# A four-stage encoder trunk: who normalises the tiles, gate-rank columns from whole x, a rounding moved, and the last norm's order

## The chip, the cores and the metric

One NeuronCore of a Trainium2 chip runs the whole program. The metric is the device time of one execution in microseconds (us).

## The reference, cut to what matters

x is 512 tokens by 1024 channels in float32. Two layers follow one another; each is a mixer and a SwiGLU network, and behind each of the four sublayers stands a norm over the channels:

```
x = layer_norm(ALPHA * x + mix(x), ln1_g, ln1_b)
x = layer_norm(ALPHA * x + swiglu(x), ln2_g, ln2_b)

h = x @ w_in                                   # even mixer
gq, gk, gv, ga, gr, sq, sk, sv = split(h)
log_a = log_sigmoid(ga @ w_a2 + b_a) / 16      # ga: 16 gate-rank columns
o = concat(gla(gq, gk, gv, log_a, gr), swa(sq, sk, sv)) @ w_out
```

The odd mixer is a gated DeltaNet with a causal convolution in front; of it only the 16 columns for beta and decay (ba) matter here.

## The kernel before, in words

**Number format.** Large products are made in three matmuls: each float32 operand is a rounded high part and a low remainder (w_hi, w_lo, x_hi, x_lo), and high x high, high x low and low x high are summed in one PSUM bank (mm3). ScalarE (ACT) rounds weights to w_hi, GpSimd (POOL) subtracts to get w_lo; both work piece by piece, two pieces to a block of 1 MB. There are two buffers for blocks, so a block may be rounded only when the block two before it is used up. The load of a block on the queue of SyncE (SP) waits for the low part of the block two before it. Only the 32 columns around the gate rank (ga) and around ba are multiplied in plain float32, by few_columns: eight contraction steps with x_hi, then eight with x_lo, in quarters of the array.

**Order.** Each engine's program is written out by hand. The eight PSUM banks are given out by unit_plan, and a result's first matmul waits until the bank's last content has been taken. TensorE (PE) computes in this order: sq, skv, gq, gk, ga, turned q and k (qT, kT), the gate matrix (a2), gv, then for each tile of 128 tokens scores, gr, attention and state; then the output projection mix, a norm, gate and up, down, a norm, and the odd layer likewise.

**The banks around gv.** qT, kT of four tiles, a2 and gv take banks in a ring. gv's tiles use banks 1, 2, 3 and 4, which held qT 1, kT 1, qT 2 and kT 2. The scores of tile 0 take banks 0 and 1, the turned k_d bank 2, and gr's tile 0 bank 3, which gv's tile 2 had. ScalarE empties all of these.

**x_tm and x_fm** are the input by tokens and by channels; they share their place in SBUF. x_fm is read at the start, x_tm is loaded over it and read by the first addition of ALPHA * x and the mixer's result.

**A norm between sublayers** (i = 1, 2, 3). For each of four tiles VectorE (DVE) adds x and the result (L1238), takes statistics of both halves (L1240, L1220); ScalarE takes the root (L841); VectorE the reciprocal (L1195), and then (x - mean) * rstd in two halves of 512 channels (L1211). The normalising of tile t - 1 is placed behind the statistics of tile t. TensorE turns each tile (turn_x, L1842, 8 transposes into 8 banks, one for each 128 channels; the last banks are those of the sublayer's last results). When the fourth tile has been turned, round_x makes x_hi and x_lo: it applies the norm's gain and bias by channel on the way out of PSUM. The first, second and third matmuls of the next block wait for it (fm_block with fresh). Just ahead of round_x, ScalarE rounds both pieces of the second weight block of the next stage.

**The last norm** (i = 4) goes to the output: VectorE computes (x - mean) * gain (L1201) and then * rstd + bias (L1206), in halves, and SP stores each half. TensorE finishes the first tile, after 12 more matmuls the second, and after 24 each the third and the fourth.

## Time and profile before

| | |
|---|---|
| median of 3 runs | 1242.6 us (1242.52 to 1243.76) |
| the profiled execution | 1242.73 us |
| its span | 1240.9 us |
| PE busy | 1226.9 us, 99% |
| DVE busy | 439.5 us, 35% |
| ACT busy | 450.8 us, 36% |
| POOL busy | 588.2 us, 47% |
| mean granted clock | 0.997 of full speed |

An engine's busy time is the union of its instructions; a matmul's duration overlaps that of the next, so the distance of two starts tells the rate. The chain of work that ended last gives PE 93% of the span and DVE 4%. In the timelines a row is: start, duration, engine, line, operation, result<-sources, how many merged, and in brackets how long the engine was idle before it and who released it.

### The profile page before, as it was taken

The page shows a single profiled execution, that of the slowest core. Times are in us where ns is not written, and L with a number is a line of the kernel's source. Part 1 is how long each engine was busy: PE and PEld are TensorE (multiplying, and loading weights), DVE is VectorE, ACT ScalarE, POOL GpSimd, SP SyncE. Part 2 cuts the span into 40 slices and gives each one's busy share as a digit, 9 for nine tenths or more (in the row PEclk, how much of TensorE's full clock was granted, in tenths as well). Part 3 has the DMA queues.
Part 4 walks back from the last instruction along what each step waited for, and adds up shares of the span by engine and source line. Part 5 has one row for each costly group of instructions (what it writes and reads, how often), then busy time and mean ns, then how long its engine had stood idle before and what let it go on. Part 6 is the DMA issues. An engine that isn't in the chain of part 4 may idle for free.

```text
span 1240.9 us, 17146 instructions
## 1 busy us (share of the span) xinstructions
PE 1226.9 (99%) x7108; PEld 1011.8 (82%) x7108; DVE 439.5 (35%) x772; ACT 450.8 (36%) x670; POOL 588.2 (47%) x280
## 2 busy tenths in 40 slices
PE   9999999999999999999999999999999999999997
PEld 7877887888888888887777888888788888888885
DVE  5556526201011100127779845654511011110105
ACT  4167825222223221215544455542532223221211
POOL 4243444943444343445744347444684444435341
PEclk9999999999999999999999999999999999999998
DMA  9322052333332333332243333124233322324221
GB/s 319 98 69 69 7 164 69 102 102 102 102 94 78 104 124 112 102 102 63 90 125 114 97 109 94 27 69 137 68 102 102 95 91 86 102 85 147 75 102 68
DMA packets 106065, 122.96 MB, mean 99 GB/s; under 512 B 18947, under 2 KB 80581, under 8 KB 105989
## 3 DMA queue, kind: packets, MB, share of 16 engines
q1 hardware_dynamic: 98244, 118.56, 29.9%
q10 hardware_dynamic: 7744, 3.32, 1.1%
q8 instruction: 56, 0.92, 0.3%
q14 instruction: 21, 0.16, 0.0%
HBM read 117.93 MB, written 3.70 MB: 98 GB/s over the span
## 4 chain that ended last, share of the span: by engine, by line
PE 93%; DVE 4%; ACT 1%; POOL 1%; DVEq 0%; ACTq 0%; issue 0%
PE bank L1666 26%; PE bank L1667 26%; PE bank L1668 26%; PE bank L2098 4%; PE bank L1697 1%; PE bank L1698 1%; PE bank L1710 1%; DVE stats L1240 1%; DVE x_tm L1238 1%; PE bank L1929 1%; PE bank L2207 1%; POOL w_lo L681 1%; PE bank L1732 1%; PE bank L2044 1%; PE bank L2190 0%; PE bank L1856 0%
## 5 line engine op out<-in xcount | busy, mean ns | idle before, releaser
L681 POOL TENSOR_TENSOR w_lo<-w_raw,w_hi 128x1024 fp32r<-128x1024 f32 (+1 forms) x200 | 470.6, 2375 | 545.8 <-ACT w_hi L816 520.9
L1666 PE MATMUL bank<-x_hi,w_hi 128*128 128x512 f32 x880 | 344.3, 391 | 0.0
L1667 PE MATMUL bank<-x_lo,w_hi 128*128 128x512 f32 x880 | 342.5, 389 | 0.0
L1668 PE MATMUL bank<-x_hi,w_lo 128*128 128x512 f32 x880 | 342.5, 389 | 0.0
L816 ACT ACTIVATE w_hi<-w_raw 128x1024 fp32r<-128x1024 f32 (+1 forms) x200 | 196.3, 1032 | 205.7 <-issue 160.4
L1666 PEld LDWEIGHTS bank<-x_hi,w_hi 128*128 128x128 f32 x880 | 165.1, 188 | 35.5 <-issue 0.8
L1668 PEld LDWEIGHTS bank<-x_hi,w_lo 128*128 128x128 f32 x880 | 165.2, 188 | 34.1
L1667 PEld LDWEIGHTS bank<-x_lo,w_hi 128*128 128x128 f32 x880 | 165.2, 188 | 33.9
L1247 DVE TENSOR_TENSOR f_ab<-bank,f_ab 128x512 f32<-128x512 f32 x44 | 30.4, 692 | 364.8 <-PE bank L1668 364.8
L1668 PE MATMUL bank<-w_hi,h_lo 128*128 128x512 f32 x352 | 136.9, 389 | 0.0
L1666 PE MATMUL bank<-w_hi,h_hi 128*128 128x512 f32 x352 | 136.9, 389 | 0.0
L1667 PE MATMUL bank<-w_lo,h_hi 128*128 128x512 f32 x352 | 136.9, 389 | 0.0
L1666 PE MATMUL bank<-w_hi,x_hi 128*128 128x512 f32 (+1 forms) x284 | 110.7, 390 | 0.7 <-POOL w_lo L681 0.7
L1238 DVE SCALAR_TENSOR_TENSOR x_tm<-x_tm,bank 128x512 f32<-128x512 f32 x32 | 22.0, 687 | 246.2 <-PE bank L1668 238.7
L1668 PE MATMUL bank<-w_hi,x_lo 128*128 128x512 f32 (+1 forms) x284 | 107.4, 378 | 0.0
L1667 PE MATMUL bank<-w_lo,x_hi 128*128 128x512 f32 (+1 forms) x284 | 107.3, 378 | 0.0
L864 ACT ACTIVATE h_hi<-f_ab 128x512 fp32r<-128x512 f32 x44 | 27.8, 632 | 187.4 <-DVE f_ab L1247 187.4
L859 ACT ACTIVATE f_ab<-bank 128x512 f32<-128x512 f32 x44 | 26.3, 598 | 144.8 <-PE bank L1668 140.5
L1666 PEld LDWEIGHTS bank<-w_hi,h_hi 128*128 128x128 f32 x352 | 66.1, 188 | 13.8
L1668 PEld LDWEIGHTS bank<-w_hi,h_lo 128*128 128x128 f32 x352 | 66.1, 188 | 13.8
L1667 PEld LDWEIGHTS bank<-w_lo,h_hi 128*128 128x128 f32 x352 | 66.1, 188 | 13.5
L1455 DVE SCALAR_TENSOR_TENSOR KH<-bank,convw,KH 128x511 f32<-128x511 f32 (+2 forms) x72 | 53.9, 749 | 26.4 <-ACT KH L1005 23.3
(297 smaller groups left out, 1257.9 us busy)
## 6 DMA issues: line engine op xcount, KB each, us to landing
w_raw<-ffn_w_gate_dram SPq DMA_DIRECT2D x22, 1024.0 KB, 5.3
w_raw<-ffn_w_up_dram SPq DMA_DIRECT2D x22, 1024.0 KB, 5.3
w_raw<-ffn_w_down_dram SPq DMA_DIRECT2D x20, 1024.0 KB, 5.0
w_raw<-od_w_in_dram SPq DMA_DIRECT2D x16, 1024.0 KB, 5.8
w_raw<-ev_w_in_dram SPq DMA_DIRECT2D x8, 1024.0 KB, 6.0
w_raw<-ev_w_out_dram SPq DMA_DIRECT2D x4, 1024.0 KB, 5.0
w_raw<-od_w_out_dram SPq DMA_DIRECT2D x4, 1024.0 KB, 5.4
x_fm<-x_fm_dram SPq DMA_DIRECT2D x8, 256.0 KB, 6.7
```

The costliest lines, as they stand in the source:

```text
L681: pool.tensor_tensor(w_lo[:, b % 2, c], w_raw[:, b % 2, c], w_hi[:, b % 2, c].bitcast(F32), ALU.subtract).then_inc(w_lo_ready, 1)
L816: act.activation(w_hi[:, i % 2, c], w_raw[:, i % 2, c], ACT.Copy).then_inc(w_hi_ready, 1)
L859: take(act.activation(f_ab[:, j, :], bank(("gate", layer, f + j))[:, :], ACT.Silu), ("gate", layer, f + j))
L864: act.activation(h_hi[:, f + j, :], f_ab[:, 2 + j, :], ACT.Copy).then_inc(s["h_hi_ready"], 1)
L1238: take(dve.scalar_tensor_tensor(cols, cols, ALPHA, bank(key)[:, :], ALU.mult, ALU.add), key)
L1240: dve.bn_stats(stats[:, t, half, :], cols).then_inc(s["half_stats"], 1)
L1247: take(dve.tensor_tensor(f_ab[:, 2 + f % 2, :], bank(("up", layer, f))[:, :], f_ab[:, f % 2, :], ALU.mult), ("up", layer, f))
L1455: ins = dve.scalar_tensor_tensor(dst, bank(key)[:, 0:SEQ - back], convw[:, tap:tap + 1], dst, ALU.mult, ALU.add)
L1666: pe.matmul(out_ap, st[0], mv_[0], start=start, stop=False)
L1667: pe.matmul(out_ap, st[0], mv_[1], start=False, stop=False)
L1668: return pe.matmul(out_ap, st[1], mv_[0], start=False, stop=stop)
L2098: return pe.matmul(o, a, b_, start=True, stop=True)
```

## The change

Six edits:

- In norms 1 to 3 ScalarE normalises tiles 0, 1 and 2: VectorE makes rstd and nm_rstd = -mean * rstd (one more small operation), and ScalarE computes rstd * x + nm_rstd in two halves, each counted on a new semaphore z_act. VectorE normalises the fourth tile alone, right behind its statistics. TensorE waits for z_act or z_norm, GpSimd for two counts of z_norm a norm in place of eight.
- Around round_x only the first piece of the second weight block is rounded ahead; the second piece is rounded behind it (split_part). In norm 2 round_x also comes ahead of three DMAs that ScalarE issues.
- few_columns for ga reads x_fm, whole float32, in eight steps. For ba it stays as it was.
- Since x_fm is now read longer, the load of x_tm waits for ga and stands behind the load of gk and both gv blocks, and ahead of the two gr blocks.
- ScalarE rounds gr's second block after the second copy of gv, no longer after the fourth.
- In the last norm the product (x - mean) * gain comes ahead of the wait for the root and of the reciprocal.

```diff
--- before.py
+++ after.py
@@ -326,6 +326,7 @@
         stats = sb("stats", [P, NT, 2, 6])
         mv = sb("mv", [P, NT, 2])
         rstd = sb("rstd", [P, NT])
+        nm_rstd = sb("nm_rstd", [P, NT])
         TH = NT * GDN_H
         ba = sb("ba", [P, NT, 2 * GDN_H])
         beta = sb("beta", [P, NT, GDN_H])
...
@@ -610,9 +611,10 @@
                       .then_inc(s["ln_landed"], 16)
 
             at = [2]
-            load_until(first_block[("gk",)])
+            load_until(first_block[("gr",)])
             low_part_there(sp, 0, KD - 2)
             low_part_there(sp, 0, KD - 1)
+            full(sp, ("ga",))
             sp.dma_start(x_tm[:, :, :], A["x"][0].rearrange("(t p) d -> p t d", p=P)).then_inc(s["x_landed"], 16)
             load_until(first_block[("gate", 0, 0)] + 1)
             taken(sp, turned(0, NT - 1, 1))
@@ -776,7 +778,7 @@
                     gate(NT - 1)
                     split_lo(b + 1, (1,))
                 if b in turned:
-                    pool.wait_ge(s["z_norm"], 2 * NT * turned[b])
+                    pool.wait_ge(s["z_norm"], 2 * turned[b])
                     split_lo(b + 1, (0,))
                     low_part_there(pool, turned[b], KD - 1)
                 if b in affine:
@@ -816,7 +818,17 @@
                         act.activation(w_hi[:, i % 2, c], w_raw[:, i % 2, c], ACT.Copy).then_inc(w_hi_ready, 1)
                     split[0] += 1
 
-            def round_x(i):
+            def split_part(b, j):
+
+                assert split[0] == b
+                if j == 0:
+                    act.wait_ge(w_landed[b % 2], 16 * (b // 2 + b % 2))
+                    act.wait_ge(*block_end[b - 2])
+                    low_weights_all(act, b - 2)
+                act.activation(w_hi[:, b % 2, pieces(b)[j]], w_raw[:, b % 2, pieces(b)[j]], ACT.Copy).then_inc(w_hi_ready, 1)
+                split[0] += j
+
+            def round_x(i, b):
 
                 gcol = 32 * ((i + 1) % 2) + 8 * ((i - 1) // 2)
                 full(act, ("xT", i, 0))
@@ -834,12 +846,21 @@
                             low_part_there(act, i, k - 4)
                         take(act.activation(f_ab[:, k % 4, :], bank(("xT", i, k))[:, :], ACT.Identity, scale=scale,
                                             bias=bias), ("xT", i, k))
-
-            def layer_norm(i):
+                split_part(b, 1)
+
+            def layer_norm(i, b=None):
                 for t in range(NT):
                     act.wait_ge(s["ln_var"], NT * (i - 1) + t + 1)
                     act.activation(rstd[:, t:t + 1], mv[:, t, 1:2], ACT.Sqrt, bias=eps[:, 0:1])\
                        .then_inc(s["ln_stat"], 1)
+                    if i < 4 and t < NT - 1:
+                        act.wait_ge(s["nm_ready"], (NT - 1) * (i - 1) + t + 1)
+                        for h in range(2):
+                            cols = x_tm[:, t, h * 512:(h + 1) * 512]
+                            act.activation(cols, cols, ACT.Identity, scale=rstd[:, t:t + 1], bias=nm_rstd[:, t:t + 1])\
+                               .then_inc(s["z_act"], 1)
+                if b is not None:
+                    split_part(b, 0)
 
             def round_o(layer, t, parts=(0, 1)):
 
@@ -929,9 +950,10 @@
             act.activation(s_p[:, 0, :, :], g_B[:, :, :], ACT.Exp, scale=-1.0 / TAU).then_inc(s["g_exp"], 1)
             split_to(first_block[("gr",)])
             for t in range(NT):
+                if t == 2:
+                    split_to(first_block[("gr",)] + 1)
                 full(act, ("gv", t))
                 take(act.activation(g_v[:, t, :], bank(("gv", t))[:, :], ACT.Copy), ("gv", t))
-            split_to(first_block[("gr",)] + 1)
 
             def copy_probs(t):
                 for g in range(KVH):
@@ -977,20 +999,18 @@
             split_to(first_block[("mix", 0, 1)])
             full(act, ("mix", 0, 0, NT - 1))
             split_to(first_block[("gate", 0, 0)])
-            layer_norm(1)
-            split_to(first_block[("gate", 0, 0)] + 1)
-            round_x(1)
+            layer_norm(1, first_block[("gate", 0, 0)] + 1)
+            round_x(1, first_block[("gate", 0, 0)] + 1)
 
             ffn(0)
             split_to(first_block[("conv", KD)])
-            layer_norm(2)
-            split_to(first_block[("conv", KD)] + 1)
+            layer_norm(2, first_block[("conv", KD)] + 1)
+            round_x(2, first_block[("conv", KD)] + 1)
 
             act.dma_start(ba_w[:, :, :], A["od_w_in"][0][:, BA0:BA0 + SB].rearrange("(k p) n -> p k n", p=P))\
                .then_inc(s["ba_landed"], 16)
             for dst, c0, n in ((o_upto, 0, P), (o_negt, P, P)):
                 act.dma_start(dst[:, :], A["c_odd"][:, c0:c0 + n]).then_inc(consts, 16)
-            round_x(2)
 
 
             def silu_conv(i):
@@ -1128,9 +1148,8 @@
             split_to(first_block[("mix", 1, 1)])
             full(act, ("mix", 1, 0, NT - 1))
             split_to(first_block[("gate", 1, 0)])
-            layer_norm(3)
-            split_to(first_block[("gate", 1, 0)] + 1)
-            round_x(3)
+            layer_norm(3, first_block[("gate", 1, 0)] + 1)
+            round_x(3, first_block[("gate", 1, 0)] + 1)
             ffn(1)
             split_to(NB - 1)
             layer_norm(4)
@@ -1191,21 +1210,24 @@
             def layer_norm(i, group, layer):
 
                 def normalise(t):
-                    dve.wait_ge(s["ln_stat"], NT * (i - 1) + t + 1)
-                    link(dve.reciprocal(rstd[:, t:t + 1], rstd[:, t:t + 1]))
                     if i == 4:
 
                         dve.wait_ge(s["ln_landed"], 32 * 4)
+                        dve.wait_ge(s["ln_var"], NT * (i - 1) + t + 1)
                         for h in range(2):
                             c = slice(h * 512, (h + 1) * 512)
                             dve.scalar_tensor_tensor(x_tm[:, t, c], x_tm[:, t, c], mv[:, t, 0:1], ln_rows[:, 0, c],
                                                      ALU.subtract, ALU.mult).then_inc(y_ready[t], 1)
+                        dve.wait_ge(s["ln_stat"], NT * (i - 1) + t + 1)
+                        link(dve.reciprocal(rstd[:, t:t + 1], rstd[:, t:t + 1]))
                         for h in range(2):
                             c = slice(h * 512, (h + 1) * 512)
                             dve.wait_ge(y_ready[t], h + 1)
                             dve.scalar_tensor_tensor(x_tm[:, t, c], x_tm[:, t, c], rstd[:, t:t + 1], ln_rows[:, 1, c],
                                                      ALU.mult, ALU.add).then_inc(y_half[t][h], 1)
                         return
+                    dve.wait_ge(s["ln_stat"], NT * (i - 1) + t + 1)
+                    link(dve.reciprocal(rstd[:, t:t + 1], rstd[:, t:t + 1]))
                     for h in range(2):
                         c = slice(h * 512, (h + 1) * 512)
                         dve.tensor_scalar(x_tm[:, t, c], x_tm[:, t, c], mv[:, t, 0:1], rstd[:, t:t + 1],
@@ -1219,12 +1241,13 @@
                             dve.wait_ge(s["half_stats"], 2 * NT * (i - 1) + NT + t + 1)
                             dve.bn_aggr(mv[:, t, :], stats[:, t, :, :].rearrange("p a b -> p (a b)"))\
                                .then_inc(s["ln_var"], 1)
-                            if i == 4:
+                            if i == 4 or t == NT - 1:
                                 normalise(t)
-                            elif t:
-                                normalise(t - 1)
-                if i < 4:
-                    normalise(NT - 1)
+                            else:
+                                dve.wait_ge(s["ln_stat"], NT * (i - 1) + t + 1)
+                                link(dve.reciprocal(rstd[:, t:t + 1], rstd[:, t:t + 1]))
+                                dve.scalar_tensor_tensor(nm_rstd[:, t:t + 1], mv[:, t, 0:1], -1.0, rstd[:, t:t + 1],
+                                                         ALU.mult, ALU.mult).then_inc(s["nm_ready"], 1)
 
             def add_sublayer(i, group, layer, half, t):
 
@@ -1722,15 +1745,15 @@
                     if k == KD - 1:
                         done(ins, keys[n])
 
-            def few_columns(key, w):
+            def few_columns(key, w, parts):
 
                 ps = fill(key)
                 quarters = P // SB
-                for j, x in enumerate((x_hi, x_lo)):
+                for j, x in enumerate(parts):
                     for k in range(KD):
                         q = k % quarters
                         ins = pe.matmul(ps[q * SB:(q + 1) * SB, :], w[:, k, :], x[:, k, :].bitcast(F32),
-                                        start=j == 0 and k < quarters, stop=j == 1 and k >= KD - quarters,
+                                        start=j == 0 and k < quarters, stop=x is parts[-1] and k >= KD - quarters,
                                         skip_group_check=True)
                 done(ins, key)
 
@@ -1836,8 +1859,10 @@
 
                 for t in range(NT):
                     for k in range(KD):
-                        if k % 4 == 0:
-                            pe.wait_ge(s["z_norm"], 2 * (NT * (i - 1) + t) + k // 4 + 1)
+                        if k % 4 == 0 and t < NT - 1:
+                            pe.wait_ge(s["z_act"], 2 * ((NT - 1) * (i - 1) + t) + k // 4 + 1)
+                        elif k % 4 == 0:
+                            pe.wait_ge(s["z_norm"], 2 * (i - 1) + k // 4 + 1)
                         ps = fill(("xT", i, k)) if t == 0 else bank(("xT", i, k))
                         ins = pe.transpose(ps[:, tile_cols[t]], x_tm[:, t, k * P:(k + 1) * P], eye[:, :])
                         if t == NT - 1:
@@ -1896,7 +1921,7 @@
                 done(pe.transpose(ps[:, 0:n], src[0:n, :], eye[0:n, 0:n]), ("const", i))
             fm_block(first_block[("gq",)], [("gq", 0), ("gq", 1)])
             fm_block(first_block[("gk",)], [("gk", 0), ("gk", 1)])
-            few_columns(("ga",), ga_w)
+            few_columns(("ga",), ga_w, (x_fm,))
             for t in range(NT):
                 ps = fill(("qT", t))
                 taken(pe, ("sq", t))
...
-                    few_columns(("ba_fm",), ba_w)
+                    few_columns(("ba_fm",), ba_w, (x_hi, x_lo))
```

ScalarE around the copies of gv. w_raw and w_hi are the weight block, bank_full4 says that gv's fourth tile is complete. Before:

```order
L816 ACTIVATE w_hi<-w_raw 128x1024 [waits w_lo_ready,w_used,w_landed1]
L816 ACTIVATE w_hi<-w_raw 128x1024
L933 ACTIVATE g_v<-bank 128x512 [waits bank_full1]
L933 ACTIVATE g_v<-bank 128x512 [waits bank_full2]
L933 ACTIVATE g_v<-bank 128x512 [waits bank_full3]
L933 ACTIVATE g_v<-bank 128x512 [waits bank_full4]
L816 ACTIVATE w_hi<-w_raw 128x1024 [waits w_lo_ready,bank_full4,w_landed0]
L816 ACTIVATE w_hi<-w_raw 128x1024
L943 ACTIVATE g_kdt<-bank 128x256 [waits bank_full2]
```

and with the change:

```order
L818 ACTIVATE w_hi<-w_raw 128x1024 [waits w_lo_ready,w_used,w_landed1]
L818 ACTIVATE w_hi<-w_raw 128x1024
L956 ACTIVATE g_v<-bank 128x512 [waits bank_full1]
L956 ACTIVATE g_v<-bank 128x512 [waits bank_full2]
L818 ACTIVATE w_hi<-w_raw 128x1024 [waits w_lo_ready,bank_full4,w_landed0]
L818 ACTIVATE w_hi<-w_raw 128x1024
L956 ACTIVATE g_v<-bank 128x512 [waits bank_full3]
L956 ACTIVATE g_v<-bank 128x512 [waits bank_full4]
L965 ACTIVATE g_kdt<-bank 128x256 [waits bank_full2]
```

The two rows of gr's second block stand between the second and the third copy, with the same wait for gv's fourth tile.

VectorE in the first norm, from the third tile's addition on. Before (the last two rows shown normalise tile 2; tile 3's pair follows after them):

```order
L1238 SCALAR_TENSOR_TENSOR x_tm<-x_tm,bank 128x512 [waits x_landed,bank_full4]
L1240 BN_STATS stats<-x_tm 128x6 [waits bank_taken4]
L1220 BN_AGGR mv<-stats 128x2 [waits half_stats]
L1195 RECIPROCAL rstd<-rstd 128x1 [waits ln_stat]
L1211 TENSOR_SCALAR x_tm<-x_tm,mv,rstd 128x512 [waits dve_step]
L1211 TENSOR_SCALAR x_tm<-x_tm,mv,rstd 128x512
L1238 SCALAR_TENSOR_TENSOR x_tm<-x_tm,bank 128x512 [waits x_landed,bank_full5]
L1240 BN_STATS stats<-x_tm 128x6 [waits bank_taken5]
L1220 BN_AGGR mv<-stats 128x2 [waits half_stats]
L1195 RECIPROCAL rstd<-rstd 128x1 [waits ln_stat]
L1211 TENSOR_SCALAR x_tm<-x_tm,mv,rstd 128x512 [waits dve_step]
```

and with the change:

```order
L1261 SCALAR_TENSOR_TENSOR x_tm<-x_tm,bank 128x512 [waits x_landed,bank_full4]
L1263 BN_STATS stats<-x_tm 128x6 [waits bank_taken4]
L1242 BN_AGGR mv<-stats 128x2 [waits half_stats]
L1248 RECIPROCAL rstd<-rstd 128x1 [waits ln_stat]
L1249 SCALAR_TENSOR_TENSOR nm_rstd<-mv,rstd 128x1 [waits dve_step]
L1261 SCALAR_TENSOR_TENSOR x_tm<-x_tm,bank 128x512 [waits x_landed,bank_full5]
L1263 BN_STATS stats<-x_tm 128x6 [waits bank_taken5]
L1242 BN_AGGR mv<-stats 128x2 [waits half_stats]
L1230 RECIPROCAL rstd<-rstd 128x1 [waits ln_stat]
L1233 TENSOR_SCALAR x_tm<-x_tm,mv,rstd 128x512 [waits dve_step]
L1233 TENSOR_SCALAR x_tm<-x_tm,mv,rstd 128x512
```

The TENSOR_SCALAR pair that stood ahead of the fourth tile's addition is gone, a small product has come behind the reciprocal, and the fourth tile's pair stands right behind its own reciprocal.

VectorE in the last norm, one tile. Before:

```order
L1220 BN_AGGR mv<-stats 128x2 [waits half_stats]
L1195 RECIPROCAL rstd<-rstd 128x1 [waits ln_stat]
L1201 SCALAR_TENSOR_TENSOR x_tm<-x_tm,mv,ln_rows 128x512 [waits ln_landed,dve_step]
L1201 SCALAR_TENSOR_TENSOR x_tm<-x_tm,mv,ln_rows 128x512
L1206 SCALAR_TENSOR_TENSOR x_tm<-x_tm,rstd,ln_rows 128x512 [waits y_ready0] x2
```

and with the change:

```order
L1242 BN_AGGR mv<-stats 128x2 [waits half_stats]
L1219 SCALAR_TENSOR_TENSOR x_tm<-x_tm,mv,ln_rows 128x512 [waits ln_var,ln_landed]
L1219 SCALAR_TENSOR_TENSOR x_tm<-x_tm,mv,ln_rows 128x512
L1222 RECIPROCAL rstd<-rstd 128x1 [waits ln_stat]
L1226 SCALAR_TENSOR_TENSOR x_tm<-x_tm,rstd,ln_rows 128x512 [waits y_ready0,dve_step]
L1226 SCALAR_TENSOR_TENSOR x_tm<-x_tm,rstd,ln_rows 128x512 [waits y_ready0]
```

The pair with mv stands ahead of the reciprocal and of its wait for ln_stat.

## Rows read from the trace of the kernel before

**Rows 1.** Chain of work that ended last, 60 to 66 us, L1732: start, us, what
```profile
61.68 3.57 PE bank L1732 x32
```

**Rows 2.** Timeline of ACT, 30 to 112 us: start, us, engine, line, operation, idle before
```profile
62.21 1.99 ACT L816 ACTIVATE w_hi<-w_raw 128x1024 fp32r<-128x1024 f32 x2
...
65.32 0.60 ACT L910 ACTIVATE g_ga<-bank 128x512 f32<-128x512 f32 x1 [1.11 <-PE bank L1732]
...
70.35 0.60 ACT L916 ACTIVATE s_qT<-bank 128x512 f32<-128x512 f32 x1
...
90.35 2.64 ACT L933 ACTIVATE g_v<-bank 128x512 f32<-128x512 f32 x4
...
92.88 2.00 ACT L816 ACTIVATE w_hi<-w_raw 128x1024 fp32r<-128x1024 f32 x2
```

**Rows 3.** Timeline of PE, gv's third tile, gv's last matmul, gr
```profile
71.00 0.50 PE L1666 MATMUL bank<-w_hi,x_hi 128*128 128x512 f32 x1
...
91.31 0.39 PE L1668 MATMUL bank<-w_hi,x_lo 128*128 128x512 f32 x1
...
92.86 0.48 PE L1666 MATMUL bank<-w_hi,x_hi 128*128 128x512 f32 x1
...
96.62 0.50 PE L1666 MATMUL bank<-w_hi,x_hi 128*128 128x512 f32 x1 [0.69 <-POOL w_lo L681]
```

**Rows 4.** Timeline of POOL, the low parts of gr's two blocks
```profile
89.40 9.51 POOL L681 TENSOR_TENSOR w_lo<-w_raw,w_hi 128x1024 fp32r<-128x1024 f32 x4 [14.80 <-ACT w_hi L816]
```

**Rows 5.** DMA issues of the span: KB each, median us to landing
```profile
x_tm<-x_dram SPq DMA_DIRECT2D x1, 2048.0 KB, 11.7
...
w_raw<-ev_w_in_dram SPq DMA_DIRECT2D x8, 1024.0 KB, 6.0
...
ba_w<-od_w_in_dram ACTq DMA_DIRECT2D x1, 128.0 KB, 2.8
```

**Rows 6.** Timeline of PE, the first norm
```profile
192.78 0.39 PE L1668 MATMUL bank<-w_hi,x_lo 128*128 128x512 f32 x1
193.01 0.93 PE L1842 MATMUL bank<-eye,x_tm 128*128 128x128 f32 x7
194.14 1.20 PE L1842 MATMUL bank<-eye,x_tm 128*128 128x128 f32 x9 [0.21 <-DVE x_tm L1238]
195.72 2.23 PE L1842 MATMUL bank<-eye,x_tm 128*128 128x128 f32 x16 [0.38 <-DVE x_tm L1211]
198.29 0.47 PE L1697 MATMUL bank<-x_hi,w_hi 128*128 128x512 f32 x1 [0.34 <-ACT x_hi L823]
```

**Rows 7.** Timeline of DVE, the first norm
```profile
193.40 0.69 DVE L1238 SCALAR_TENSOR_TENSOR x_tm<-x_tm,bank 128x512 f32<-128x512 f32 x1
...
196.23 1.00 DVE L1211 TENSOR_SCALAR x_tm<-x_tm,mv,rstd 128x512 f32<-128x512 f32 x2
197.33 0.81 DVE L1177 TENSOR_SCALAR f_ab<-bank,lnc 128x512 f32<-128x512 f32 x1
```

**Rows 8.** Timeline of ACT, the first norm
```profile
195.29 1.99 ACT L816 ACTIVATE w_hi<-w_raw 128x1024 fp32r<-128x1024 f32 x2
...
197.37 0.78 ACT L823 ACTIVATE x_hi<-bank,lnc 128x512 fp32r<-128x512 f32 x1
198.18 0.63 ACT L826 ACTIVATE x_hi<-f_ab 128x512 fp32r<-128x512 f32 x1
```

**Rows 9.** Timeline of DVE, the last norm, first tile and start of the second
```profile
1218.27 0.69 DVE L1238 SCALAR_TENSOR_TENSOR x_tm<-x_tm,bank 128x512 f32<-128x512 f32 x1 [42.34 <-PE bank L1668]
...
1219.72 0.21 DVE L1220 BATCH_NORM_AGGREGATE mv<-stats 128x2 f32<-128x12 f32 x1
1220.30 0.16 DVE L1195 RECIPROCAL rstd<-rstd 128x1 f32<-128x1 f32 x1 [0.36 <-ACT rstd L841]
1220.49 1.41 DVE L1201 SCALAR_TENSOR_TENSOR x_tm<-x_tm,mv,ln_rows 128x512 f32<-128x512 f32 x2
...
1223.33 0.69 DVE L1238 SCALAR_TENSOR_TENSOR x_tm<-x_tm,bank 128x512 f32<-128x512 f32 x1
```

2 lines of the change are left out of this document (1 added, 1 removed).

## The prediction

> **What bounds the kernel now.** I read first the busy shares (the table above): TensorE is busy nearly the whole span, so the kernel is one stream of matmuls, and an edit can only gain where it shortens that stream, closes one of the few holes in it, or shortens what comes behind it. The view of waits then says where the holes are. So I read three places in time order: the gate-rank columns and the gr weights (61 to 98 us), the norm between two sublayers (193 to 198 us; it comes three times, and the norms at 557 and 867 us have the same rows within 0.02 us), and the last norm (1218 us on), where TensorE is done and the VectorE chain sets the end.
>
> **Gate-rank columns.** few_columns for ga ran 32 matmul records in 3.57 us [rows 1], 0.112 each. With x_fm alone 16 are left: TensorE is 1.79 us shorter. That doesn't all arrive. The kernel's next work needs banks that ScalarE empties, in order: g_ga, s_qT, s_kT, with the rounding of gv's second block in the middle. The g_ga copy starts at 65.32, but ScalarE is busy with gv's first weights until 64.20 [rows 2], so it comes forward by 1.05 only. The third tile of gv needs the bank of the third s_qT copy, out at 70.35 + 0.60 = 70.95 [rows 2], and TensorE takes it at 71.00 [rows 3]: no slack. So gv is 1.05 us earlier, not 1.79, and the rest is a new wait of 0.7 in front of that tile.
>
> **The rounding moved.** Before, ScalarE copied four gv tiles (90.35, 2.64 us) and then rounded gr's second block (92.88) [rows 2]. Now that rounding stands between the second and the third copy, and it waits for gv's last tile, because it overwrites a weight buffer that gv reads. gv's last matmul starts at 91.31 and takes 0.39 [rows 3], so gv is full at 91.70 before, 90.65 now. Then come 2.00 us of rounding and 0.66 of copy: bank 3 is free at about 93.4. The first gr matmul needs that bank. It started at 92.86 [rows 3] and could now start at 91.8. It will wait some 1.6 us and start at 93.4, 0.5 later than before. What the move pays for is the wait behind it: TensorE stood 0.69 us (0.85 by the starts of the matmuls) before 96.62 for the low part of gr's second block [rows 3], the third of four pieces that GpSimd makes in 2.38 us each from 89.40 on [rows 4]. The high part of that piece is now there at 91.75 instead of 93.9. GpSimd's first two come at least the 1.05 us earlier that the gate's matmuls do, so the low part is ready at 89.40 - 1.05 + 3 x 2.38 = 95.5 or before. TensorE reaches it at 93.4 + 2.9 = 96.3 and does not wait. Net for the front: 96.62 to 96.3, **0.3 us gained**. Bounds: 1.0 lost, if low half or a bank comes later still; 2.5 gained, if nothing holds (1.79 + 0.69).
>
> **The moved x_tm load.** It now waits on SP for ga (about 63.5) and stands in front of both gr blocks. 11.7 us for x_tm and 6.0 for each block [rows 5], taken one after the other, give 75.2, 81.2 and 87.2. The first block's rounding takes 2 us right ahead of the copies at 90.35 [rows 2], so it began at 88.3; it could come 7 us earlier and find its weights. The second can't start before 90.65 and has 3.5 us. x_tm itself is read only after all of gr. Cost nothing; without that cover each us late is a us lost.
>
> **The three norms.** Before, 32 transposes follow the last matmul: 7 from 193.01, then a wait of 0.21, since the eighth bank was still held by VectorE's late addition of the fourth tile; 9 from 194.14; a wait of 0.38 for tile 2's normalising; 16 from 195.72 [rows 6]. At 0.13 each the fourth tile starts at 195.72 + 8 x 0.13 = 196.77. VectorE did the fourth addition at 193.40 though its matmul was over at 192.78 + 0.39 = 193.17 [rows 6, 7], since it was normalising. Now ScalarE normalises tiles 0 to 2. Its nearest rows are 0.78 for 512 columns with a scale and a bias, and 0.63 for a copy from SBUF [rows 8]; I take 0.78. Twelve matmuls of 0.227 from start to start (192.78 to 193.01) part the tiles, so tile 2's addition starts at 193.20 - 2.72 = 190.5, and with 0.7 each for addition and statistics and 0.2 for the aggregate it is out at about 192.1; root, reciprocal and the product -mean x rstd are done by 192.75, and both halves by 194.35. TensorE needs them at 195.1. The addition of tile 3 starts at 193.20, frees the bank at 193.9 when transpose 8 asks, and its chain (0.7 + 0.7 + 0.2 + 0.3 + 0.15) has the first half normalised at 195.85. So 24 transposes run from 193.01 without a hole to 196.2: the fourth tile starts 0.57 earlier. From there the order is as before: VectorE's f_ab for the second bank (197.33), ScalarE's second rounding (198.18), which holds TensorE's third matmul [rows 7, 8]. ScalarE's first rounding started at 197.37, right behind 1.99 us of weight rounding; half of that is now behind, so it isn't late either. **0.57 gained in each, 1.7 in three.** Bounds for each: 0.2, if another producer is next; 0.93, all that TensorE waits there (0.21 + 0.38 + 0.34 [rows 6]). What is moved behind is hidden: the second weight piece is wanted by GpSimd only after the last x_lo, and the three DMAs that ScalarE issues in the second norm (ba_w among them) now stand behind its rounding. ba_w takes 2.8 us to land [rows 5] and is read after the 48 matmuls (10.9 us) that follow the first rounding. Rounding is 8.6 us; the weight piece another 1.05. If the DMA waited for both to end, TensorE would lose up to 0.5 us; if ScalarE's queue issues it ahead of them, nothing. I take nothing and keep 0.5 as a bound.
>
> **The last norm.** Per tile VectorE did add, statistics, aggregate (until 1219.93), waited for the root, took the reciprocal at 1220.30, and then two and two products; the next tile began at 1223.33, 5.06 after 1218.27 [rows 9]. The first products don't need the root. They start now at 1219.96, and the reciprocal (0.16, with its step 0.19) stands between the pairs. Saved is the wait: 1220.30 - 1219.95 = 0.35 a tile. The pitch becomes 4.71, the fourth tile starts at 1218.27 + 3 x 4.71 = 1232.4, still after TensorE's last matmul (behind the first tile's come 12 + 24 + 24 more: 1218.2 + 60 x 0.227 = 1231.9), so VectorE stays the bound and all four count: **1.4 gained**. Bounds 0.8 (the product waits on its own engine's aggregate) and 2.1 (the reciprocal hides too, 0.53 a tile).
>
> **Sum.** 0.3 + 1.7 + 1.4 = 3.4 us. The profiled execution took 1242.73 (span 1240.9), the median of the runs is 1242.6; I go from the median: **1239.2**. A measurement of this kernel can tell 0.2%, 2.5 us, from no change.
>
> **Rivals.**
> - *The front gives all.* If the third s_qT copy and the third gv copy don't hold TensorE (another order of banks than I read), 1.79 and 0.69 arrive: 2.5 + 1.7 + 1.4 = 5.6, 1237.0. Against it: the 71.00 start right behind 70.95. Chance 0.14.
> - *The edits overlap or are swallowed.* The hold in front of gr is longer than the wait it removes by up to 1 us, or the norms give 0.2 each because the transposes are followed by the same chain: 0.3 to 2.5 gained, some 1240.8. For it: three of four terms are differences of waits of 0.2 to 0.7 us. Chance 0.17.
> - *Slower: ScalarE too slow for normalising.* Each tile comes 2.72 us after the one before, and root plus two halves must fit. At 0.78 they fit (1.9). From about 1.5 us a half they don't: tile 2 ends at 196.5, and the root of tile 3 stands behind it on ScalarE. At 1.8 a half the fourth tile's transposes start at 199.1 instead of 196.8, 2.3 lost in each norm, 6.9 - 0.3 - 1.4 = 5.2 in all: 1247.8. Against it, 0.78 and 0.63 [rows 8]. Chance 0.04. The Trainium skill speaks for this side (ScalarE: Activation LUTs, Rules for kernel authors): multiplications and additions belong on VectorE, not ScalarE. The trace agrees on the price, 1.00 us for VectorE's two halves [rows 7] against 2 x 0.78, but ScalarE waits there over 2 us a tile for statistics, so the dearer engine is the free one.
> - My forecast, 2.5 to 4.7 gained: chance 0.65.
>
> **Range.** 1236.9 takes in the full front, 1241.1 most of the swallowed case: 1236.9 to 1241.1. Faster is 0.65 + 0.14 and 0.02 from the swallowed case's upper end, 0.81; same the rest of that case and the lightest 0.01 of the slower one, 0.16; slower 0.03.
>
> **What would show it.** few_columns for ga with 16 records in 1.8 us. A wait of TensorE for ScalarE's g_v at the first gr matmul (about 1.6 us), one of 0.7 in front of gv's third tile, and none for w_lo there. In each norm, transposes without a hole until the fourth tile, and the first gate (or conv) matmul some 5.0 us after the last one of the sublayer, ScalarE's x_tm at about 0.78 a half. At the end a pitch of 4.7. I am wrong in the front if TensorE doesn't wait for g_v, in the norms if the way from last matmul to first remains 5.5, at the end if the pitch falls to TensorE's own.

## The result and the profile after

The changed kernel takes **1246.0 us** (median of 9 runs, 1245.61 to 1246.61); the kernel before, run beside it, 1242.97 (9 runs, 1242.51 to 1243.76). The ratio is 1.0025, 95% interval 1.0016 to 1.0033. The changed kernel is slower by 3.0 us; the forecast was 3.4 faster, and 1246.0 lies above the range. The profiled execution took 1246.61 with a span of 1244.8, before 1242.73 with 1240.9: the spans differ by 3.9. The granted clock is 0.997 before and 0.998 after, the upper of its two levels.

I cut both spans by starts of TensorE's instructions in its timeline (us, from one mark to the next; stages whose length did not change are left out):

| from - to | before | after |
|---|---|---|
| start - first matmul of ga | 61.61 | 61.46 |
| ga - first attention of tile 0 | 36.59 | 36.17 |
| - first transpose, norm 1 | 94.81 | 94.75 |
| - first gate matmul (norm 1) | 5.28 | 4.59 |
| down of layer 0, first to last matmul | 119.46 | **122.96** |
| transposes to conv (norm 2) | 5.27 | 4.48 |
| odd mixer, turned qkv to turned output | 51.32 | **52.35** |
| transposes to gate 1 (norm 3) | 5.27 | 4.59 |
| down of layer 1 | 119.46 | **122.96** |
| start of the last matmul - end | 9.48 | 8.0 |

Everything that the forecast named got shorter. What got longer are two stages that it did not name: down, twice 3.50 us, and the odd mixer, 1.03 us.

These are the groups of instructions of TensorE of the changed kernel, shapes kept apart (busy us in all, mean ns of one, idle before): two of the three groups of the gate and up matmuls, and below them down's. The first source is the operand that streams (128x512), the second the one that is loaded (128*128):

```profile
L1691 PE MATMUL bank<-x_hi,w_lo 128*128 128x512 f32 x880 | 342.5, 389 | 0.0
L1690 PE MATMUL bank<-x_lo,w_hi 128*128 128x512 f32 x880 | 342.5, 389 | 0.0
...
L1691 PE MATMUL bank<-w_hi,h_lo 128*128 128x512 f32 x352 | 139.2, 396 | 0.0
L1690 PE MATMUL bank<-w_lo,h_hi 128*128 128x512 f32 x352 | 139.2, 395 | 0.0
L1689 PE MATMUL bank<-w_hi,h_hi 128*128 128x512 f32 x352 | 139.2, 395 | 0.0
```

and down's groups of the kernel before:

```profile
L1668 PE MATMUL bank<-w_hi,h_lo 128*128 128x512 f32 x352 | 136.9, 389 | 0.0
L1666 PE MATMUL bank<-w_hi,h_hi 128*128 128x512 f32 x352 | 136.9, 389 | 0.0
L1667 PE MATMUL bank<-w_lo,h_hi 128*128 128x512 f32 x352 | 136.9, 389 | 0.0
```

The same 1056 instructions with the same shapes and nothing idle in front of them take 6.6 ns more each: by the marks 7.0 us / 1056. Gate and up did not change: 389 ns in both, 391 for their third group. The diff has no line in down's code. But it has one that moves down's operands: `nm_rstd = sb("nm_rstd", [P, NT])` needs 16 bytes of each partition, and sb rounds every tile up to 32. They lie in front of the arena (the stretch of SBUF that the mixers' buffers and h share), so h_hi and h_lo, down's rounded input and its remainder, and all behind them stand 32 bytes further than before, while the weights' and x's tiles keep their place.

TensorE's timeline after, at the places of the forecast (start, duration, engine, line, what, idle before):

```profile
61.46 1.92 PE L1755 MATMUL bank<-x_fm,ga_w 128*32 128x512 f32 x16
...
69.81 0.50 PE L1689 MATMUL bank<-w_hi,x_hi 128*128 128x512 f32 x1 [0.55 <-ACT s_qT L937]
...
93.32 0.50 PE L1689 MATMUL bank<-w_hi,x_hi 128*128 128x512 f32 x1 [1.42 <-ACT g_v L956]
...
192.38 4.26 PE L1867 MATMUL bank<-eye,x_tm 128*128 128x128 f32 x32
196.97 0.47 PE L1720 MATMUL bank<-x_hi,w_hi 128*128 128x512 f32 x1 [0.34 <-DVE f_ab L1196]
...
733.66 0.69 PE L2123 MATMUL bank<-blocks_in,GA 32*32 32x32 f32 x32 [0.90 <-issue]
```

They answer to [rows 1, 3, 6]: half of the ga matmuls are gone, a short wait for s_qT and one of 1.42 for g_v have come, the wait for w_lo at the fourth gr group is gone; the 32 transposes of norm 1 run in one piece; and a wait of 0.90 has come in the odd mixer, which has none before.

ScalarE in the front and in norm 1 (answers to [rows 2, 8]), then GpSimd's low parts [rows 4] and VectorE in norm 1 [rows 7]:

```profile
64.13 0.60 ACT L931 ACTIVATE g_ga<-bank 128x512 f32<-128x512 f32 x1
...
84.45 1.99 ACT L818 ACTIVATE w_hi<-w_raw 128x1024 fp32r<-128x1024 f32 x2
...
90.59 2.00 ACT L818 ACTIVATE w_hi<-w_raw 128x1024 fp32r<-128x1024 f32 x2 [0.81 <-PE bank L1691]
92.67 1.28 ACT L956 ACTIVATE g_v<-bank 128x512 f32<-128x512 f32 x2
...
192.63 1.52 ACT L860 ACTIVATE x_tm<-x_tm,nm_rstd,rstd 128x512 f32<-128x512 f32 x2 [0.42 <-DVE nm_rstd L1249]
```

```profile
85.58 4.85 POOL L683 TENSOR_TENSOR w_lo<-w_raw,w_hi 128x1024 fp32r<-128x1024 f32 x2 [12.00 <-ACT w_hi L818]
91.72 4.71 POOL L683 TENSOR_TENSOR w_lo<-w_raw,w_hi 128x1024 fp32r<-128x1024 f32 x2 [1.29 <-ACT w_hi L818]
```

```profile
192.69 0.69 DVE L1261 SCALAR_TENSOR_TENSOR x_tm<-x_tm,bank 128x512 f32<-128x512 f32 x1
...
194.92 1.00 DVE L1233 TENSOR_SCALAR x_tm<-x_tm,mv,rstd 128x512 f32<-128x512 f32 x2
196.02 0.81 DVE L1196 TENSOR_SCALAR f_ab<-bank,lnc 128x512 f32<-128x512 f32 x1
```

The last norm on VectorE, first tile and start of the second [rows 9]:

```profile
1223.23 0.69 DVE L1261 SCALAR_TENSOR_TENSOR x_tm<-x_tm,bank 128x512 f32<-128x512 f32 x1 [43.76 <-PE bank L1691]
...
1224.68 0.21 DVE L1242 BATCH_NORM_AGGREGATE mv<-stats 128x2 f32<-128x12 f32 x1
1225.01 1.41 DVE L1219 SCALAR_TENSOR_TENSOR x_tm<-x_tm,mv,ln_rows 128x512 f32<-128x512 f32 x2
1226.34 0.15 DVE L1222 RECIPROCAL rstd<-rstd 128x1 f32<-128x1 f32 x1
...
1228.04 0.69 DVE L1261 SCALAR_TENSOR_TENSOR x_tm<-x_tm,bank 128x512 f32<-128x512 f32 x1
```

### The profile page after: what moved, and what is told of

Read it like the earlier page. It is cut to its first block, busy times and chain, and to the rows that moved or that the text cites. A ratio compares the mean times of both kernels' runs of the same rounds, so it can differ in the third digit from the quotient of the medians.

```text
span 1244.8 us, 17127 instructions
## 1 busy us (share of the span) xinstructions
PE 1231.3 (99%) x7092; PEld 1011.3 (81%) x7092; DVE 432.4 (35%) x763; ACT 464.4 (37%) x688; POOL 588.2 (47%) x280
## 2 busy tenths in 40 slices
DMA packets 106064, 122.96 MB, mean 99 GB/s; under 512 B 18946, under 2 KB 80580, under 8 KB 105988
## 4 chain that ended last, share of the span: by engine, by line
PE 95%; DVE 2%; ACT 1%; issue 1%; DMA 0%; ACTq 0%; DVEq 0%
PE bank L1689 27%; PE bank L1690 27%; PE bank L1691 27%; PE bank L2123 4%; PE bank L1720 1%; PE bank L1721 1%; PE bank L1733 1%; DVE x_tm L1261 1%; PE bank L1867 1%; PE bank L1954 1%; PE bank L2232 1%; DVE stats L1263 1%; PE bank L2069 0%; PE bank L2215 0%; PE bank L1881 0%
## 5 line engine op out<-in xcount | busy, mean ns | idle before, releaser
L818 ACT ACTIVATE w_hi<-w_raw 128x1024 fp32r<-128x1024 f32 x194 | 190.4, 1031 | 212.2 <-issue 165.2
L1689 PEld LDWEIGHTS bank<-w_hi,x_hi 128*128 128x128 f32 x284 | 53.5, 188 | 12.8 <-ACT g_v L956 1.7
```

What stands on the lines that cost most here:

```text
L818: act.activation(w_hi[:, i % 2, c], w_raw[:, i % 2, c], ACT.Copy).then_inc(w_hi_ready, 1)
L1689: pe.matmul(out_ap, st[0], mv_[0], start=start, stop=False)
```

## Experiments

### Where h stands

The theory: the place of h_hi and h_lo in SBUF sets the rate of down's matmuls, and 32 bytes cost 7 us by themselves. The rival: something in the change that runs beside down (another order on ScalarE or on the queues) slows it. The first four kernels move buffers, in the changed kernel and in the one before. Each is one line:

```
e1, after,  behind nm_rstd:      +        pad = sb("pad", [P, 8])
e2, before, behind rstd:         +        pad = sb("pad", [P, 8])
e3, before, behind rstd:         +        pad = sb("pad", [P, 16])
e4, after,  in front of h_hi:    +        pad = sb("pad", [P, 8])
```

**e1.** 

> The changed kernel with 32 unused bytes a partition behind the new nm_rstd, so that everything behind it, h_hi and h_lo among it, lies again at a multiple of 64 bytes as before the change. Theory A (the place of the arena: nm_rstd takes 32 bytes and moves it from a multiple of 64 to 32 beyond one, and the matmuls that read h run at 0.2333 us from start to start instead of 0.2267): the two down stages take 119.5 us again instead of 123.0, and the time is 1246.0 - 7.0 = 1239.0, or 1238 if the 1.1 us that the odd mixer lost have the same cause. Theory B (the slower stretch comes from something else in the change, the program's layout or the work that ScalarE got): 1246.0 as the changed kernel, down 123.0.

**e2.** 

> The kernel before with 32 unused bytes a partition behind rstd, where the change put nm_rstd; nothing else. Theory A: both down stages go from 119.5 to 123.0 us, and the time from 1243.0 to 1250, 1251 with the odd mixer's share. Theory B: 1243.0.

**e3.** 

> The kernel before with 64 unused bytes at the same place: everything behind moves, but stays at multiples of 64. Theory A, in the form that only the place within 64 bytes counts: 1243.0, down 119.5. If the place within 128 bytes counts, or moving alone costs: about 1250. Theory B: 1243.0.

**e4.** 

> The changed kernel with the 32 bytes only in front of h_hi, so that h_hi, h_lo, ln_rows and f_ab lie at multiples of 64 again, and the buffers of both mixers stay 32 beyond one. Theory A: down 119.5 us, time 1239.0; the odd mixer (conv's first matmul to the first transpose of norm 3) stays 1.1 us longer than before, if that has to do with the place of its own buffers, and e1 is that much faster than this one. Theory B: 1246.0.

Measured (before beside them: 1243.01; e3 has two runs): e1 1246.41 (ratio 1.0026, 1.0015 to 1.0037), e2 1249.95 (1.0054, 1.0039 to 1.0069), e3 1249.56 (1.0051, 1.0031 to 1.0071), e4 1246.49 (1.0025, 1.0015 to 1.0036). A down stage takes 122.96 or 122.97 us in each of the four. So the rival falls: the kernel before, with nothing but 32 unused bytes, loses 6.9 us. And with h at 64 bytes instead of 32 nothing comes back, so it isn't that h has to stand at a multiple of 64.

The second four ask whether a larger unit of h's place counts, or its distance from something, and what the change does when no buffer moves:

```
e5, before, in front of h_hi:    +        pad = sb("pad", [P, 32])
e6, after:   -        rstd = sb("rstd", [P, NT])
             -        nm_rstd = sb("nm_rstd", [P, NT])
             +        norms = sb("norms", [P, 2, NT])
             +        rstd = norms[:, 0, :]
             +        nm_rstd = norms[:, 1, :]
e7, before, between h_hi, h_lo:  +        pad = sb("pad", [P, 8])
e8, before:  -        base = (nc.sbuf_base + 63) // 64 * 64
             +        base = (nc.sbuf_base + 63) // 64 * 64 + 32
```

**e5.** 

> The kernel before with 128 unused bytes a partition in front of h_hi alone, so that h_hi, h_lo, ln_rows and f_ab move and nothing else does. The place of h was good at 0 and slow at 32 and 64 beyond it. Theory A1 (a matmul that loads h as its stationary operand is slow unless h lies at a multiple of 128 bytes): both down stages 119.5 us, time 1243.0. Theory A2 (what counts is a larger unit, 256 or 512 bytes, or the distance to the weights): 123.0 and 1250.0.

**e6.** 

> The changed kernel with nm_rstd in the 16 bytes a partition that rstd left unused, so that no buffer moves against the kernel before. Theory A (place of h): both down stages 119.5 us, time 1246.0 - 7.0 = 1239.0, and 1238.2 if the odd mixer is back at its length. Theory B (the change's work itself slows the down stages): 1246.0.

**e7.** 

> The kernel before with 32 unused bytes between h_hi and h_lo: h_hi stays at its place, h_lo, ln_rows and f_ab move. One matmul in three loads h_lo. If each matmul pays for its own stationary operand: down 119.5 + 3.5 / 3 = 120.6 us, time 1245.3. If the place of h_hi alone counts (two matmuls in three): 119.5 and 1243.0. If one misplaced operand slows all three: 123.0 and 1250.0.

**e8.** 

> The kernel before with every buffer 32 bytes further, so that distances stay and places change. Theory A1 (the place of the stationary operand itself): all large matmuls, not only down's, start 0.2333 us apart; some 5100 of them by 0.0066 give 34 us, 1277. Theory A3 (the distance between h and the weight buffers counts, not the place): 1243.0, down 119.5. Only h is sensitive, for a reason of its own: 1250.0.

Measured (before beside them: 1242.78; e5, e7 and e8 ran once, and their down stages, equal in both layers to 0.01 us, carry the argument): e5 1248.34 in one run, 122.47 a down stage; e6 **1239.66** (9 runs, 1239.13 to 1240.47; ratio 0.9974, 0.9964 to 0.9984), 119.45; e7 1249.39 in one run, 122.96; e8 1242.7 in one run, 119.46.

e8 is the telling one: there every buffer stands 32 bytes further and nothing is lost. So not h's place counts but its distance from other operands. e7 left h_hi in place and moved only h_lo; its down groups:

```profile
L1668 PE MATMUL bank<-w_lo,h_hi 128*128 128x512 f32 x352 | 140.8, 400 | 0.0
L1667 PE MATMUL bank<-w_hi,h_hi 128*128 128x512 f32 x352 | 139.0, 395 | 0.0
L1669 PE MATMUL bank<-w_hi,h_lo 128*128 128x512 f32 x352 | 137.0, 389 | 0.0
```

From start to start the three take 239, 233 and 228 ns, before 226 or 227 each. It is not the product that reads h_lo that is slow, but the one before it in the order of mm3, w_lo x h_hi at 400 ns: while that one runs, the next one's 128 x 128 operand is loaded (in this trace the load starts within 0.01 us of the matmul and takes 188 ns), and that operand is h_lo. This suggests that the load and the running matmul get in each other's way, though the 395 ns of w_hi x h_hi, with both tiles and the next load in place, don't fit it. The next job tries that, and the unit.

```
e9, before, in front of w_lo and of h_lo:  +        pad = sb("pad", [P, 8])
    and ones and eps in one tile (32 bytes back, so that h_hi keeps its place):
             -        ones = sb("ones", [P, 1])
             -        eps = sb("eps", [P, 2])
             +        one_eps = sb("one_eps", [P, 3])
             +        ones = one_eps[:, 0:1]
             +        eps = one_eps[:, 1:3]
e10, before, in front of h_hi:   +        pad = sb("pad", [P, 128])
e11, before, in front of h_hi:   +        pad = sb("pad", [P, 64])
```

**e9.** 

> The kernel before with w_lo and the tiles behind it 32 bytes further, h_hi in its old place (ones and eps share 32 bytes to make room) and h_lo 32 bytes further: h_hi against w_hi and h_lo against w_lo as before, h_hi against w_lo and h_lo against w_hi moved. Theory D1 (what counts is the stationary tile that is loaded beside the moving one that streams, and in the order hi-hi, hi-lo, lo-hi that is h_hi beside w_hi and h_lo beside w_lo): 119.46 us for a down stage, 1242.8 in all. Theory D2 (what counts is a matmul's own two tiles): both mixed products are out of place, at or above 123.0 a stage, 1249.5 or more. Theory D3 (the distance from h_hi to h_lo): 123.0, 1249.5. If x against the weights' tiles counts as well, the gate and up stages (239.60 us) get longer too, and the time goes beyond 1255.

**e10.** 

> The kernel before with 512 bytes in front of h_hi alone. If distances count by their rest in some unit of at most 512 bytes: 119.46 us a down stage and 1242.8 in all. If the unit is larger: near 122.5 to 123.0, 1248 to 1249.5.

**e11.** 

> The kernel before with 256 bytes in front of h_hi alone. Unit of at most 256 bytes: 119.46 us a down stage, 1242.8. Unit of 512 or more: 122 to 123, 1248 to 1249.5.

Measured (before: 1243.05): e9 **1268.96** (two runs, ratio 1.0207, 1.0188 to 1.0225); e10 1243.17 (1.0, 0.999 to 1.001), 119.45 a down stage; e11 1242.73 (0.9997, 0.9987 to 1.0007), 119.45. So 256 and 512 bytes cost nothing where 32, 64 and 128 did: as far as these five tell, what counts is the rest of a distance in 256 bytes. D1, my theory of the pair of e7, is refuted in the form in which I put it: h_hi against w_hi and h_lo against w_lo stood as before, and a down stage took 122.38. The groups of e9:

```profile
L1669 PE MATMUL bank<-x_hi,w_hi 128*128 128x512 f32 x880 | 351.1, 399 | 0.0
L1670 PE MATMUL bank<-x_lo,w_hi 128*128 128x512 f32 x880 | 349.1, 397 | 0.0
L1671 PE MATMUL bank<-x_hi,w_lo 128*128 128x512 f32 x880 | 345.9, 393 | 0.0
L1669 PE MATMUL bank<-w_hi,h_hi 128*128 128x512 f32 x352 | 139.1, 395 | 0.0
L1671 PE MATMUL bank<-w_hi,h_lo 128*128 128x512 f32 x352 | 138.9, 395 | 0.0
L1670 PE MATMUL bank<-w_lo,h_hi 128*128 128x512 f32 x352 | 138.4, 393 | 0.0
```

Here x and w_lo stand 32 bytes off w_hi, and the gate and up matmuls, at 389 to 391 ns in every other kernel, take 393 to 399: their stage is 246.59 us instead of 239.60, in both layers. All kernels together, as rests in 256 bytes counted from w_hi:

| kernels | h_hi | h_lo | w_lo, x | down stage, us | gate and up, us |
|---|---|---|---|---|---|
| before, e6, e8, e10 to e18 | 0 | 0 | 0 | 119.45 - 119.46 | 239.6 |
| changed, e2 | 32 | 32 | 0 | 122.96 | 239.6 |
| e1, e3, e4 | 64 | 64 | 0 | 122.96 - 122.97 | 239.6 |
| e5 | 128 | 128 | 0 | 122.47 | 239.6 |
| e7 | 0 | 32 | 0 | 122.96 | 239.6 |
| e9 | 0 | 32 | 32 | 122.38 | 246.6 |

Wherever all operands of a stage have one rest, the rate is full; wherever one has another, the stage is 2.4 to 2.9% longer (122.38 / 119.46, 122.96 / 119.46). Which two accesses meet inside the engine is not settled by this; nor were other rests (96, 160, 192, 224) tried.

**e16** is the changed kernel with its own nm_rstd and h_hi 256 bytes from its old place, all small tiles behind nm_rstd still moved:

```
+        pad = sb("pad", [P, 56])
         h_hi = sb("h_hi", [P, KF, SEQ], F32R)
```

> The changed kernel with nm_rstd in its own 32 bytes and 224 bytes more in front of h_hi alone, which then stands 256 bytes behind its place in the kernel before; all small tiles and f_ab behind stay moved. If the matmul's rate goes by the rest of the distance in 256 bytes: 119.46 us a down stage, 1239.7 in all, as with no buffer moved (1239.66). If any other moved buffer has a part in the 7 us: above 1240.5.

Measured: 1239.81 (1239.19 to 1240.71; ratio 0.9974, 0.9964 to 0.9985), 119.46 and 119.45 a down stage. The other moved buffers have no part in what down lost.

### What each part of the change brings

With e6, the parts alone, in the kernel before, no buffer moved (before beside them: 1242.85). Their edits are the hunks of the change: e13 those of load_until, few_columns and the rounding in gv's copies; e14 the order in `normalise` for i == 4; e15 `layer_norm`, `round_x` and `split_part` for i < 4, nm_rstd beside rstd as in e6.

**e13.** 

> The kernel before with the front part alone (gate-rank columns from x_fm, the rounding of gr's second block ahead of gv's third copy, the load order on SP's queue); no buffer moves. Forecast's term: 0.3 us faster. By the milestones of the changed kernel: PE's last matmul of the front 0.3 to 0.6 earlier, 1242.4 to 1242.7.

**e14.** 

> The kernel before with the last norm's order alone (x minus mean times weight ahead of the reciprocal of the deviation); no buffer moves. Forecast's term: 1.4 us faster, 1241.6. If the output's store, and not VectorE, ends the kernel: under 0.5 faster, 1242.5 or more.

**e15.** 

> The kernel before with the first three norms alone (three tiles normalised by ScalarE, the fourth by VectorE), nm_rstd in the 16 bytes that rstd leaves unused. Forecast's term: 3 x 0.57 = 1.7 us faster, 1241.3; by the milestones of the changed kernel 3 x 0.7 = 2.1, 1240.9. If parts of it are given back later in the odd mixer: 1241.5 or more, with the time from the first transpose of qkv to the first of the output over 51.32.

Measured: e13 1242.68 (ratio 0.9997, 0.9987 to 1.0007), e14 1241.91 (0.9992, 0.9983 to 1.0002), e15 1241.34 (0.9984, 0.9975 to 0.9994). As differences of medians 0.17 + 0.94 + 1.51 = 2.6 us, against 3.1 with all three (e6: 1242.78 - 1239.66). Singly, only e15's gain is certain by its interval. The stages are sharper than the whole, since the moment at which ga starts differs by up to 1.2 us between profiles (61.40 to 62.64), with and without the front part. So e14's gain shows from the last matmul's start to the end, 8.44 against 9.48. From the first ga matmul to the first attention of tile 0, the thirteen kernels without the front part take 36.59 to 36.66, six with it 36.17 or 36.18 (the seventh, e12, follows).

The next two take the front apart:

```
e12, as e6, and one row later:   -                if t == 2:
                                 +                if t == 3:
e17, before: only the hunk of load_until(first_block[("gr",)]) and full(sp, ("ga",))
e18, before: only  if t == 3: split_to(first_block[("gr",)] + 1)  inside the loop over gv's copies
```

**e12.** 

> The changed kernel with nm_rstd in the 16 bytes that rstd leaves unused (no buffer moves, 1239.66 us measured) and the second block of gr rounded ahead of the fourth copy of gv instead of the third. If the wait of 1.42 us for g_v at gr's first matmul is the third tile's copy behind the rounding: the wait is gone, and of it 0.9 to 1.4 us arrive, 1238.3 to 1238.8. If the wait only moves (to w_lo, 0.69 before, or to the fourth tile): 1239.0 to 1239.7.

**e17.** 

> The kernel before with the x_tm load moved alone on SP's queue (behind gv's blocks and ga's full bank, in front of gr's). Forecast: nothing, 1242.8, no wait of TensorE in the front. If the load's place is what lengthens the round trip of the blocks in the odd mixer: 9.5 to 10.1 us from the store's issue to the reload's instead of 8.86, and up to 0.9 us slower.

**e18.** 

> The kernel before with the rounding of gr's second block alone moved, ahead of gv's fourth copy (as in the kernel that came out fastest). Theory: the wait of 0.69 us for w_lo goes and no wait for g_v takes its place, 0.5 to 0.7 us faster, 1242.1 to 1242.4, round trip of the blocks 8.4 to 9.1 us. Rival: a wait for g_v at gr's first matmul or at the fourth copy's user takes its place, 1242.8.

e12: **1238.39** (5 runs, 1237.51 to 1238.52; ratio 0.9959, 0.9946 to 0.9973). It is the fastest of all, 4.7 us under the kernel before and 1.3 under e6, as the theory had it (0.9 to 1.4). Its front takes 34.48 instead of 36.17, which is 1.69 less and beyond the theory; the odd mixer took 0.30 of it back (51.80 against 51.50 in e6). On TensorE's timeline the first gr matmul now stands without any wait.

```profile
91.77 0.44 PE L2007 MATMUL bank<-eye,g_kd 128*128 128x128 f32 x2
91.96 0.48 PE L1690 MATMUL bank<-w_hi,x_hi 128*128 128x512 f32 x1
```

ScalarE has copied gv's third tile by then and rounds behind it; the fourth copy, the only one now behind the rounding, has a user that comes late enough.

e17: 1242.89 (ratio 0.9999, 0.9989 to 1.0008), front 36.62. The load's new place costs nothing, as forecast. e18: 1243.13 (1.0001, 0.9992 to 1.001), front 36.60: the theory missed, and so did its rival. The old wait is still there,

```profile
97.52 0.50 PE L1667 MATMUL bank<-w_hi,x_hi 128*128 128x512 f32 x1 [0.68 <-POOL w_lo L681]
```

since GpSimd makes its four low parts in one row from 90.28 on, whenever the rounding comes:

```profile
90.28 9.53 POOL L681 TENSOR_TENSOR w_lo<-w_raw,w_hi 128x1024 fp32r<-128x1024 f32 x4 [14.81 <-ACT w_hi L816]
```

### The odd mixer

In the profiles of all seven kernels with the front part (the changed one, e1, e4, e6, e12, e13, e16) the way of a set of small blocks out to device memory and back, in the odd mixer, takes 9.47 to 10.07 us from the first store's issue to the first reload's, in the other thirteen 8.40 to 9.13. On SP's queue after:

```profile
717.89 0.51 SPq L641 DMA_DIRECT2D t_blocks<-OO  x1
718.45 0.43 SPq L643 DMA_DIRECT2D t_blocks<-M  x1
727.95 3.79 SPq L654 DMA_DIRECT2D blocks_in<-t_blocks  x8
```

and before:

```profile
716.47 0.51 SPq L639 DMA_DIRECT2D t_blocks<-OO  x1
717.02 0.43 SPq L641 DMA_DIRECT2D t_blocks<-M  x1
725.33 3.79 SPq L652 DMA_DIRECT2D blocks_in<-t_blocks  x8
```

10.06 against 8.86. The reload waits until both stores have landed, and it is the second store that is later: t_blocks<-M (512 KB) lands 9.48 us after its issue, before 8.29, and the weight block issued 0.96 us ahead of it takes 7.93 instead of 6.71; the first store is little changed (7.64, 7.18). In the seven the second store takes 8.91 to 9.50 and that block 7.36 to 7.95, in the other thirteen 7.83 to 8.56 and 6.30 to 6.97. The mixer takes 51.50 to 52.35 us in those seven and 51.32 to 51.42 in the others I cut so (e9, slowed throughout, apart). Neither the load alone (e17, 8.43) nor the rounding alone (e18, 9.13) does it, and e13 shows that the front part does it without the norms (9.47, a mixer of 51.61). What is left is ga's half columns or parts of the front together. How an edit at 62 us lengthens a transfer at 717 stays open.

## Why the prediction was wrong

**The step that failed is the list of parts.** The forecast costed few_columns, the rounding, the x_tm load, the norms and the last norm; the line that allocates nm_rstd had no term at all, not even one of nothing with its cover named. It cost 7.0 us in the two down stages and 6.2 to 6.9 in the whole, twice what all the rest gained: e2 shows it alone (1249.95 against 1243.01), e6 and e16 show the change without it (1239.66 and 1239.81, where 1239.2 was forecast). That these two come so near to the forecast is in part luck: of its terms the norms were 0.3 us too low in sum, the front 0.1 too low and the last norm 0.3 too high, and the odd mixer was not in it.

**Gate-rank columns and the rounding**: 0.3 forecast, 0.42 measured (36.59 to 36.17). The chain is as forecast: 16 records instead of 32, g_ga copied at 64.13 instead of 65.32 (1.19 earlier, 0.15 of it the earlier start of ga; 1.05 was said), a wait of 0.55 for the third s_qT where 0.7 was said, gr's first matmul at 93.32 (about 93.4 was said) after 1.42 of wait (1.6), no wait for w_lo. One reason was wrong: I took that wait to be paid by the rounding's move. e18 moves the rounding alone and keeps the wait; in the changed kernel GpSimd starts its low parts at 85.58 instead of 89.40 [rows 4], 3.8 us earlier and not 1.05. Its pieces follow ScalarE's rounding, and that follows a chain between VectorE and ScalarE whose first link, the gate's bank, came 1.87 us earlier (68.92 to 67.05), with ga's shorter columns. The other 1.95 us are in the next link, VectorE's first product of the gate; before and after:

```profile
69.71 2.64 DVE L1301 SCALAR_TENSOR_TENSOR g_kd<-g_B 128x512 f32<-128x512 f32 x1
```

```profile
67.84 0.69 DVE L1324 SCALAR_TENSOR_TENSOR g_kd<-g_B 128x512 f32<-128x512 f32 x1
```

Before, this product starts while GpSimd makes a low part (69.39 to 71.80) and ends 0.55 us behind that part; after, it starts ahead of GpSimd's part (68.21) and isn't stretched. The second product starts beside a low part in both, takes 1.9 us and ends 0.55 behind it too. The first takes 0.69 in all seven kernels with the front part and 2.62 to 2.65 in the thirteen others. The forecast had no such term. I did not try ga's half columns without the rounding.

**The x_tm load** cost nothing (e17), and the ba_w DMAs nothing either: from norm 2's conv to the turned qkv 151.08 us against 151.05.

**The norms**: 0.57 each forecast; 0.69, 0.79 and 0.68 measured, 0.67 to 0.69 each in e6; the 0.1 more in norm 2, which follows down, goes with down's slower matmuls (e2, with the old norms, takes 5.13 there instead of 5.27). The 32 transposes run without a hole, ScalarE's half takes 0.76 (1.52 for two) where 0.78 was taken from [rows 8], and the fourth tile's addition, at 192.69, is 0.31 behind the first transpose instead of 0.39 [rows 6, 7], right behind its matmul. The last wait stays, 0.34, for f_ab instead of x_hi. What follows the transposes came forward with them: ScalarE's first x_hi starts at 195.88, 3.50 behind the first transpose, before 4.36 [rows 6, 8]; that gave some 0.1 more than the fourth tile's own 0.57. The rule of the Trainium skill (ScalarE: Activation LUTs, Rules for kernel authors) that additions and multiplications belong on VectorE holds for the price here, 0.76 against VectorE's 0.50 a half, and not for the choice: e15 is 1.5 us faster.

**The last norm**: 1.4 forecast, 1.0 to 1.1 measured at full rate (from the last matmul's start to the end of the span 9.48 before, 8.39 in e6, 8.44 in e14). The pitch is 4.81, not 4.71. The first product starts 0.33 behind the aggregate's start (1224.68, 1225.01) where I took 0.24, so it does wait for its own engine's aggregate; the bound of 0.8 had named that. In the changed kernel the tail is 8.0, since the slower matmuls put 60 x 0.0066 = 0.4 us of it ahead of the last matmul.

**The odd mixer** took back 1.03 us (0.18 in e6). No term of the forecast stands for it.

**The rivals.** The slower one came true in sign and not in kind: ScalarE is not too slow, its halves take 0.76 in 2.7 us a tile. The swallowed case did not come: the front gave 0.42 and each norm 0.67 or more, where it had a loss and 0.2. The rival in which the front gives all (2.5) was dismissed for the changed kernel rightly; e12 shows that it was one row of code away, at 36.59 - 34.48 = 2.1.

## What to carry to other kernels

Read the diff for what it allocates, not only for what it executes: on a kernel that TensorE bounds, list the address of each large matmul operand before and after, and where they no longer agree in their rest by 256 bytes, reckon with the 2.4 to 2.9% that these stages lost, and put the small buffer elsewhere or in bytes that another leaves unused. Compare groups of equal instructions by their mean duration first: one that the diff doesn't touch and that is 6 ns dearer 1056 times is the whole result here. A rounding or a copy that is moved ahead for one consumer should be placed by the first bank that it holds back; one row later gave 1.3 us.
